# Where the six modulation vectors are summed: MLP scales later, MLP gate on VectorE, none in the first output stage

## The reference, cut to what matters

```python
def ada_modulation(cond, w, b):
    m = jax.nn.silu(cond) @ w + b                 # w: 2048 x (6*2048)
    return jnp.split(m[..., None, :], N_MOD, axis=-1)

sh_a, sc_a, g_a, sh_m, sc_m, g_m = ada_modulation(c, w_ada[layer], b_ada[layer])
csh_a, csc_a, cg_a, csh_m, csc_m, cg_m = ada_modulation(c_ctx, w_ada[layer], b_ada[layer])
...
x = x + g_a * (jnp.concatenate([attn, pool], axis=-1) @ w_out[layer])
hm = modulate(rms_norm_2(x, norm_mlp_w[layer]), sh_m, sc_m)    # h*(1+scale)+shift
x = x + g_m * squared_relu_mlp(hm, w_mlp_up[layer], w_mlp_down[layer])
```

## Time and profile before

| | |
|---|---|
| runs before | 1814.24 us median of 3 (1813.35 to 1815.23) |
| profiled execution | 1812.95 us, span 1811.3 us |
| mean granted TensorE clock | 0.965 of full |
| PE busy | 1671.5 us, 92% |
| DVE busy | 1050.5 us, 58% |
| ACT busy | 759.0 us, 42% |
| POOL busy | 31.5 us, 2% |
| DMA | 374.71 MB, mean 207 GB/s |
| matmuls of L441 (modulation rows) | 102.2 us busy, x768 |
| loads of `ada_raw` | x96, 1 MB each, 6.5 us from issue to landing (median) |

### The profile page before, as it was taken

One profiled execution on the slowest core, in us unless ns is written; L12 is line 12 of the kernel. 1 busy time (PEld: TensorE's weight loads), 2 busy tenths in 40 slices (PEclk: granted clock), 3 DMA queues, 4 the chain that ended last, 5 costly groups with the idle time before them and its releaser, 6 DMA issues.

```text
span 1811.3 us, 34903 instructions
## 1 busy us (share of the span) xinstructions
PE 1671.5 (92%) x12462; PEld 1508.9 (83%) x12462; DVE 1050.5 (58%) x1568; ACT 759.0 (42%) x1068; POOL 31.5 (2%) x48
## 2 busy tenths in 40 slices
PE   3899999899988986999889869999999999999996
PEld 2788888788877876878779859989998999899985
DVE  4445454455556557467665575655556555555675
ACT  5344444334333334344344434434443454345442
POOL 0000000000000000000000000000000000000000
PEclk9899999899998998999999969999999999999998
DMA  7677777688874775673225515555555555555552
GB/s 311 242 268 251 276 269 258 214 302 288 301 283 167 286 258 192 256 291 117 94 70 175 176 68 185 185 186 181 180 186 192 183 183 186 185 184 183 185 189 92
DMA packets 88370, 374.71 MB, mean 207 GB/s; under 512 B 10256, under 2 KB 10768, under 8 KB 75488
## 3 DMA queue, kind: packets, MB, share of 16 engines
q1 hardware_dynamic: 87120, 369.54, 59.0%
q0 software_dynamic: 1168, 4.00, 0.7%
HBM read 371.40 MB, written 2.10 MB: 206 GB/s over the span
## 4 chain that ended last, share of the span: by engine, by line
issue 72%; PE 16%; DVE 8%; ACT 3%; POOL 0%; DVEq 0%; ACTq 0%; POOLq 0%
PE G L400 4%; PE G L401 4%; PE G L402 4%; DVE lo L1050 3%; ACT hi L731 1%; PE ADA L441 1%; PE M L624 1%; PE S L611 1%; PE ADA L638 1%; PE S L598 1%; DVE t L1097 0%; DVE resid L1512 0%; DVE sm L1344 0%; DVE blk L1050 0%; PE S L599 0%
## 5 line engine op out<-in xcount | busy, mean ns | idle before, releaser
L1050 DVE TENSOR_TENSOR lo<-raw,hi 128x1024 fp32r<-128x1024 f32 x496 | 607.8, 1225 | 427.9 <-ACT hi L731 396.1
L400 PE MATMUL G<-actA,hi 128*128 128x256 f32 x2368 | 691.8, 292 | 31.7 <-DVE actA L1050 31.1
L731 ACT ACTIVATE hi<-raw 128x1024 fp32r<-128x1024 f32 x496 | 525.6, 1060 | 387.3 <-PE G L427 194.6
L401 PE MATMUL G<-actA,lo 128*128 128x256 f32 x2368 | 676.5, 286 | 0.0
L402 PE MATMUL G<-actA,hi 128*128 128x256 f32 x2368 | 676.2, 286 | 0.0
L400 PEld LDWEIGHTS G<-actA,hi 128*128 128x128 f32 x2368 | 458.6, 194 | 93.0 <-issue 73.9
L401 PEld LDWEIGHTS G<-actA,lo 128*128 128x128 f32 x2368 | 459.2, 194 | 0.4
L402 PEld LDWEIGHTS G<-actA,hi 128*128 128x128 f32 x2368 | 458.7, 194 | 0.0
L426 PE MATMUL G<-actB,hi 128*128 128x512 f32 x1024 | 358.6, 395 | 0.0
L427 PE MATMUL G<-actB,lo 128*128 128x256 f32 x1024 | 287.5, 281 | 0.0
L426 PEld LDWEIGHTS G<-actB,hi 128*128 128x128 f32 x1024 | 192.2, 188 | 44.5
(11 more groups left out here) (173 smaller groups left out, 1004.8 us busy)
## 6 DMA issues: line engine op xcount, KB each, us to landing
raw<-stream_dram SPq DMA_DIRECT2D x496, 512.0 KB, 4.2
ada_raw<-w_ada_dram SPq DMA_DIRECT2D x96, 1024.0 KB, 6.5
x_tok<-x_tok_dram SPq DMA_DIRECT2D x1, 2048.0 KB, 8.3
resid<-xT_dram SPq DMA_DIRECT2D x1, 2048.0 KB, 10.9
ctx_tok<-ctx_tok_dram SPq DMA_DIRECT2D x1, 2048.0 KB, 17.9
W<-ctxT_dram POOLq DMA_DIRECT2D x16, 128.0 KB, 6.1
out_dram<-resid SPq DMA_DIRECT2D x4, 512.0 KB, 2.6
ada_raw<-pool_w_dram POOLq DMA_DIRECT2D x1, 1024.0 KB, 6.9
```

What stands on the lines that cost most here:

```text
L400: pe.matmul(bank, hi[:, slot, cols], x[:, k, 0:T], start=(k == 0), stop=False, skip_group_check=True)
L401: pe.matmul(bank, lo[:, slot, cols], x[:, k, 0:T], start=False, stop=False, skip_group_check=True)
L731: return act.activation(dst, src, ACT.Copy)
L1050: return dve.tensor_tensor(dst, a, b, op)
```

## The change: what it does

Block 4 takes the place of block 5 in the key, value and query units, and starts two units earlier there: its 16 rows stand behind units 81 to 87, one each, then four in step 0, four in step 1 and one in step 2. The turn of block 4 stays where that of block 5 was, in step 3; the copy on ACT that it needs moves from step 3 to the end of step 2. The units of the first output stage have no modulation row.

Block 5 is not summed by PE's wide matmuls. Its 16 MB come as 16 loads of 1 MB in another layout, 128 partitions by 4 pieces of 512 columns, into one slot, one for each lap of two down units in MLP groups 0 and 1. DVE adds each, multiplied by one column of `cpad` per partition, to an array `gate_part` of 128x2048 (`scalar_tensor_tensor`, sixteen in all), cleared by GpSimd after unit 104. At the start of group 3 PE sums `gate_part` over the partitions with 16 matmuls of one column (`gate_sums`), and DVE adds the bias.

```diff
+SCALE_LOADS = {U_KV + 2: 1, U_KV + 3: 1, U_KV + 4: 1, U_KV + 5: 1, U_KV + 6: 1, U_KV + 7: 2,
+               U_Q: 2, U_Q + 1: 2, U_Q + 2: 2, U_Q + 3: 1}
...
+        gate_part = W[:, 1024:3072]
+        gate_raw, gate_c = ada_raw[:, 0], cpad[:].rearrange("p k n -> p (k n)")
...
             for u in range(U_KV, U_OUT2):
-                for _ in range(1 if U_KV + 4 <= u < U_Q else 2 if U_Q <= u < U_Q + 6 else 0):
-                    if e < KT:
-                        ada_load(5 * KT + e, e % 2, ada_used, 5 * KT + e - 1)
-                        e += 1
+                for _ in range(SCALE_LOADS.get(u, 0)):
+                    ada_load(4 * KT + e, e % 2, ada_used, 4 * KT + e - 1)
+                    e += 1
...
+            def gate_load(k):
+
+                m, g = divmod(k, 4)
+                src = ada_w[5 * KT:6 * KT].rearrange("(n m) p (g c) -> m g p n c", m=4, g=4)[m, g]
+                if k:
+                    sp.wait_ge(gate_taken, 1 * k)
+                sp.dma_start(gate_raw, src).then_inc(gate_full, 16)
...
+                for i in range(8):
+                    gate_load(8 * g + i)
+                    at = U_MLP + 2 * KT * g + KT + 2 * i
+                    for n in range(2 * at + 8, 2 * at + 12):
+                        weight(n % RING, n)
...
+            pool.wait_ge(w_used, 2 * U_OUT2 + 2)
+            pool.memset(gate_part, 0.0).then_inc(gate_zero, 1)
...
             for n in range(UNITS_OUT):
-                unit(At(U_OUT1), n, actB, inB, ada=U_OUT1 + n)
+                half_unit(At(U_OUT1), n, 0, actB, inB)
+                if n == 0:
+                    ada_turn()
+                half_unit(At(U_OUT1), n, 1, actB, inB)
...
             at = At(U_KV)
-            half_unit(at, 0, 0, actC, inC)
-            ada_turn()
-            half_unit(at, 0, 1, actC, inC)
+            unit(at, 0, actC, inC)
...
                 if s < 3:
-                    ada_rows(5 * KT + 4 + 4 * s)
-                    ada_rows(5 * KT + 5 + 4 * s)
+                    ada_rows(4 * KT + 7 + 4 * s)
+                if s < 2:
+                    ada_rows(4 * KT + 8 + 4 * s)
...
-                if s < 3:
-                    ada_rows(5 * KT + 6 + 4 * s)
-                    ada_rows(5 * KT + 7 + 4 * s)
+                if s < 2:
+                    ada_rows(4 * KT + 9 + 4 * s)
+                    ada_rows(4 * KT + 10 + 4 * s)
...
+            def gate_sums():
+
+                pe.wait_ge(gate_taken, KT)
+                for m in range(KT):
+                    x = pe.matmul(S[0][:, m:m + 1], gate_part[:, m * P:(m + 1) * P], ones[:, 0:1], start=(m == 0), stop=(m == KT - 1),
+                                  skip_group_check=True)
+                x.then_inc(gate_summed, 1)
...
+                    with turn.lap(dve, 8, "dve gate down") as i:
+                        for j in range(2):
+                            down(At(base + KT, 2, i), j, bass.ds(i * 2 + j, 1), True, None)
+                        dve.wait_ge(gate_full, i * 16 + 16 * (8 * g + 1))
+                        dve.scalar_tensor_tensor(gate_part, gate_raw.rearrange("p k n -> p (k n)"),
+                                                 gate_c[:, bass.ds(i * 38 + (8 * 38 * g + 6), 1)], gate_part,
+                                                 ALU.mult, ALU.add).then_inc(gate_taken, 1)
```

More of the change, by code:

```diff
@@ L68 @@
     "dve down": {"seq": 2, "lo_done": 4},
+    "dve gate down": {"seq": 2, "lo_done": 4, "gate_taken": 1},
     "dve last down": {"seq": 4, "lo_done": 4, "sqs": 2, "sq_added": 2},
@@ L235, in program @@
         inP = sem("inP")
+        gate_zero, gate_full, gate_taken, gate_summed = (sem(n) for n in ("gate_zero", "gate_full", "gate_taken", "gate_summed"))
         out_ready, out_sent = sem("out_ready"), sem("out_sent")
@@ L291, in _ @@
             ada(1, 1, first=True)
-            with sp.Fori(0, U_KV // 4 - 1) as i:
+            with sp.Fori(0, U_OUT1 // 4) as i:
                 for j in range(4):
@@ L992, in _ @@
                 split(at, 2 * s + 1)
+                if s == 2:
+                    ada_copy(4)
                 if s == 0:
@@ L1496, in _ @@
                 else:
+                    dve.wait_ge(gate_summed, 1)
+                    seq(tt(adav[:, 0, G_M:G_M + KT], S[0][:, 0:KT], col("b_ada", 5 * KT, KT), ALU.add))
                     with turn.lap(dve, 7, "dve last down") as i:
```

54 lines of the change are left out of this document (31 added, 23 removed).

## The result

The changed kernel takes 1821.55 us in the median of 6 runs (1820.14 to 1822.50), the kernel before, run beside it, 1814.38 (1813.35 to 1815.23). The ratio is 1.0039, with a 95% interval of 1.0026 to 1.0052: **slower by 7.2 us**. The forecast was 1810.8, with a range of 1806.5 to 1815.5.

What follows compares the result with a forecast made beforehand. A loop of DVE and ACT was taken to bound the first output stage, PE the MLP. Terms -1.0 - 3.6 - 0.96 - 1.5 + 3.6 = -3.5 us took the median from 1814.24 to 1810.8 us, range 1806.5 to 1815.5.

Steps and rivals of the forecast that it cites:

- Gate loads: MLP down groups 0 and 1: each load lands in the median 6.5 us, wanted after 8.5 us, so 0 us.
- the rival: Late gate loads, MLP down groups 0 and 1: each lap takes landing plus 2.8 us; 33 us at longest landing; chance 0.06.
- Sums, +3.6: Start of MLP group 3: the 16 fp32 sums, 32 passes, add 3.6 us on PE, the bound there.
- Output stage, -1.0: First output stage: without rows only the wait in unit 65 goes, -1.0 us; the DVE and ACT loop then bounds.
- End of the stage, -3.6: End of first output stage: without block 4's turn the norm starts 4.6 us earlier, 1.0 already counted, so -3.6 us.
- The three rows in the key and value units: Ahead of units 82 to 84: 3.6 us of rows, hidden while PE waits for DVE's norm tiles.
- Query stage, -0.96 and -1.5: Query stage: one row fewer ahead of unit 93 gives -0.96 us; the earlier copy gives -1.5 us in step 3.
- the clock falls: Rival: new PE pauses bring the low clock; hidden in the output stage, some 3 us in query step 3; chance 0.11.
- Gate on DVE, 2.8 us, hidden: MLP down groups 0 and 1: DVE's new operation takes 2.8 us, bounds 2.4 and 3.9, hidden, 0 us.
- Other pace: Rival: moved code changes the pace of down stages, 1.7 us apart; -6.9 to -0.1 in all; chance 0.12.

Runs made afterwards that it cites:

- e2: The changed kernel without the 16 gate loads and the waits for them; DVE still adds what lies in the slot: 1815.41 us.
- e3: The changed kernel with the gate's weights laid out so each load reads one 8 KB piece per partition: 1815.64 us.
- e10: The changed kernel with the sums in four portions and two slots for the gate loads, pieces still 2 KB: 1820.90 us.
- e1: The changed kernel without the gate's loads, DVE additions and sums; the gate is only its bias: 1809.08 us.
- e12: e3 with its 16 one-column sums replaced by four matmuls of 512 columns: 1813.09 us.
- e5: The changed kernel with 8 KB pieces for the gate loads and the 16 sums in four places: 1809.96 us.
- e8: The kernel before, with modulation rows 65 to 79 multiplying 32 columns instead of 512: 1813.59 us.
- e7: The kernel before, with the turn of block 4 moved later and ACT's copy of block 5 moved to the end of query step 2: 1808.81 us.
- e11: e5 with four extra matmuls, whose results nobody reads, in step 3 of the query stage: 1808.04 us.
- e6: The kernel before, with only the turn of block 4 (and its bias addition) moved later, into unit 81: 1812.21 us.
- e9: e7 with three of block 5's rows moved into the key and value units and one row ahead of unit 93 instead of two: 1807.30 us.

## Why the prediction was wrong, point by point

**The step that failed** is "Gate loads": "Loads of this size took 4.8 to 11.6 us, 6.5 in the median ... I take the median: 0 us." The allowance of 8.5 us (8.9 with DVE's measured 2.35) and the point from which it decides, a landing of 9.5 us, hold. The landing was 9.3 to 10.4 us, 9.6 in the median, in the first group and 9.2 to 10.0 in the second, and the two down stages grew by 6.4 us; without the loads (e2) the time is 6.1 us less. The same sentence had the warning, "Pieces of 2 KB don't occur in the trace", and yet took a value from rows of 8 KB pieces. e3 shows that the layout is the reason, size and places of the pieces together. What the trace gave was a price for another kind of transfer, so the rival deserved far more than 0.06. The Trainium skill, "Perfetto Trace Analysis", section "DMA Optimizations", says that batching small transfers, such as 2 KB into 4 or 8 KB, can improve the throughput dramatically; the runs agree, with 9.6 against 7.0 us for the same 1 MB, as far as the size is what counts in e3, and the prediction should have weighed this rule. The rival's mechanism was the right one: a lap became landing and DVE's operation in turn, 12.7 us. It named the weights behind the load only as a help; in e10 they stall PE by themselves, once a stage, behind two loads in a row. Its 33 us came from the longest landing, 11.6, in every lap, which did not occur.

**Sums, +3.6: a term that was mis-sized.** Their 32 passes took 4.05 us, the last of them at the low clock, where 3.6 were forecast. But the term had no place for what comes behind them: the first matmuls of group 3 ran at 0.50. From the sums to the end of the last unit the changed kernel lost 6.6 us, and the stages give the parts: 4.05 for the sums, 2.56 in the up stage behind them, and the pace, which takes 1.7 off down stage 2 and puts 1.7 on down stage 3. In e2 against e1 it is 3.49, 1.56 and 1.69 of pace, which nothing pays back there. So length, low clock and pace together make the whole. e12 shortens the up stage by 1.2 with the clock alone. Spread in four, the sums cost 2.3 us of MLP time (e1 to e5), less than their length, as down stage 3 has the fast pace in e5 and the slow one in e1.

**Output stage, -1.0.** The mechanism was right (e8, and the period of 7.76 us in all three kernels). The size was 0.4: the stage is 0.37 us shorter. The other 0.6 went ahead of the wait, as DVE's additions for units 64 and 65 show, of the changed kernel and then for unit 64 of the kernel before:

```profile
565.13 0.42 DVE L1091 TENSOR_TENSOR resid<-resid,G 128x256 f32<-128x256 f32 x1 [4.16 <-issue]
...
572.29 0.42 DVE L1091 TENSOR_TENSOR resid<-resid,G 128x256 f32<-128x256 f32 x1
...
564.45 0.42 DVE L1050 TENSOR_TENSOR resid<-resid,G 128x256 f32<-128x256 f32 x1 [3.58 <-issue]
```

The wait of 1.0 us at unit 65 is gone, as forecast. But PE ran unit 64 at the low clock until 564.6 instead of 563.2, and so the first addition, from which the loop starts, came 0.7 us later, 0.6 of it against the start of the stage.

**End of the stage, -3.6.** Right. Unit 80 started 0.26 us earlier and the norm 3.90, so this part gave 3.64. Together with the stage's own 1.0 it was to be 4.6; unit 86 was 4.35 us earlier. The three rows in the key and value units cost nothing, as forecast.

**Query stage, -0.96 and -1.5.** The first is 0.87 by PE's start of unit 93. The second was there (1.48 in e7, 1.4 in e11), but the changed kernel lost it to the low clock. This is the rival "the clock falls", right in place, at half the size that it gave: some 3 us, where step 3 lost 1.6 against e7. In the output stage, where that rival had pauses and slow halves too, PE paused by up to 1.42 us in a period and the clock stayed at 1.00. The forecast gave the rival 0.11, though the same row that stood behind it, the pause at 714.4 in the earlier trace rows, was known. The rule of the Trainium skill cited there, "TensorE: Matmul & The Clock Gate", "What's actually happening", that activity releases the throttle, agrees with e11, where extra work for PE kept the clock at 1.00 and made the query stage 1.0 us shorter. It agrees with e12 only if activity is not the same as being busy.

**Gate on DVE, 2.8 us, hidden.** Hidden, yes (e2). Its length was 2.35 us, a little under the lower bound of 2.4.

**Not foreseen, +1.7.** The second output stage and the first up stage are 0.5 and 1.2 us longer, in e1 to e5 as well, and not in e6 to e9. In e11 the output stage is 0.9 us longer than before, the up stage no longer. In the trace the granted clock is low from 1032 to 1056 and again from 1060 to 1070, before from 1038 to 1072. The gate's loads and sums are not the cause, since e1 has neither. Two low stretches instead of one don't make the loss by themselves either: e6 has them too (1036.7 to 1053.8 and 1057.2 to 1070.8), and its up stage takes 105.84. What is the cause was not tried alone.

**Other pace: the sizes right, the reason wrong.** The prediction put the two paces of the down units (90.5 and 88.8 us a stage) down to where their code lies. In the changed kernel the same loop of down stage 0 runs at 2.83 us a half unit before one of its stalls, at 2.77 after it, and at 2.83 again after another. Code doesn't move within a loop, so where it lies can't be all of it: the pace changes with a stall. In all, the down stages of e1 take as long as before's (358.6 us for the four), only with the paces dealt out the other way round. So it was never a gain or loss of 6.9 between these two. In the changed kernel down stage 3 has the slow pace and down stage 2 the fast one, before it was the other way round, so it adds nothing to the loss from the sums on. But e2 has three slow stages and e3 too, e5 one, and before two, so comparisons between single kernels carry 1.7 us for each. What sets the pace at a stage's start stays open.

## What to carry to other kernels

Price a transfer by rows with the same pieces, in size and place, not with the same total; where no such row exists, lay the data out so that the known row applies, or measure, and count what queues behind it besides what waits for it. A second buffer can hide a late landing, but look at what two such transfers in a row do to those behind them.

Where one engine's clock follows its activity, taking work from beside the bound makes pauses, and the first work behind a pause may be slow. A gain of a us or two behind such a pause is safe only if the pause is short or filled. Put narrow matmuls between wide ones in small groups instead of in one run.

And take a change apart before judging it. Here the turn and the copy alone made the kernel 5.2 us faster, and the gate's move took 12.5.

## What the runs showed of the hardware that was not expected

- One MB in 512 pieces of 2 KB (four for each partition, 4 MB apart, 8 KB from partition to partition) landed in 9.2 to 10.4 us, and in 4.8 to 7.7 us as 8 KB rows in one stretch, with the same weights around it. With two slots, and so sometimes two such loads in flight, it took up to 15.4 us.
- PE fully busy with one-column fp32 matmuls (4.05 us of them, 3.49 in e2 and e3) goes from clock 1.00 to 0.50 while they run or 0.7 us behind them; with matmuls of 512 columns over 3.03 us it stays at 1.00.
- The same code with the same pause of 2.33 us ahead of it ran at full clock in the kernel before and at 0.50 in e6; a later step with a pause of 2.21 us shows the same pair. Pauses of up to 1.42 us in each period of the output stage left the clock at 1.00. So a pause makes the low clock possible, and whether it comes depends on something else as well, perhaps on when the pause falls.
- Down units run at 2.83 or 2.77 us a half unit, and a stall can switch from one to the other.
- `scalar_tensor_tensor` on DVE in fp32 took 2.35 us for 128x2048. That is 1.04 ns for each element beyond 256 (485 ns), where the short forms of the earlier trace rows had given 1.27.
